# The activation buffers act_hi and act_lo moved up by 23872 bytes in each partition, the small buffers down by 32768

## What is computed

```
h = rmsnorm(x); x = x + nsa_pool_mixer(h, ...)      # q, k, v panels, three attention branches, pooling
x = x + swiglu(rmsnorm(x), w_gate, w_up, w_down)    # hidden width 2816
x = x + conformer_conv(rmsnorm(x), ...)             # 1024 -> 2048, depthwise conv of 31, layernorm, 1024 -> 1024
x = x + swiglu(rmsnorm(x), ...)
x = rmsnorm(x)                                      # end of the first block
u = _rmsnorm(h); proj = u @ w_in                    # q, k, v, g, and three conv inputs
h = h + concat([gla(...), conv(...)]) @ w_out
h = h + (silu(a) * b) @ w_down                      # a, b = _rmsnorm(h) @ w_gate_upffn
h = h + sigmoid(_rmsnorm(h) @ w_ple_gate) * (p @ w_ple_proj)
return _rmsnorm(h)
```

## Time and profile before

| | us |
|---|---|
| median of 3 runs | 1786.94 |
| lowest and highest | 1786.29 to 1790.84 |
| the profiled execution, its own time | 1790.93 |
| its span, first to last instruction | 1789.1 |
| PE busy | 1734.1 (97%) |
| DVE busy | 1251.9 (70%) |
| ACT busy | 867.4 (48%) |
| POOL busy | 516.9 (29%) |
| granted TensorE clock, mean | 0.979 |

### The profile page before, as it was taken

The page is one execution under the profiler, slowest core; times in us unless marked ns, Lnnn a source line. Parts: engine busy times, 40 slices in busy tenths (PEclk is TensorE's granted clock), DMA queues, the critical chain, the costliest instruction groups (busy, mean ns, idle before and its releaser), DMA issues.

```text
span 1789.1 us, 27531 instructions
## 1 busy us (share of the span) xinstructions
PE 1734.1 (97%) x10662; PEld 1498.1 (84%) x10662; DVE 1251.9 (70%) x1756; ACT 867.4 (48%) x1310; POOL 516.9 (29%) x356
## 2 busy tenths in 40 slices
PE   8999999999999999899999999999999999999997
PEld 6777788988998866689988998788788998899876
DVE  8667677754785798688744776678857875477575
ACT  5337556732773322456732763443335673277342
POOL 1342115502540246225502540012301550254000
PEclk9798999999999999899999999999999999999998
DMA  6210133333333465223333332422212333333332
GB/s 214 82 47 1 62 81 95 95 107 106 95 91 98 120 153 145 74 80 95 99 103 106 95 103 87 123 72 71 71 64 78 95 95 106 106 95 94 107 93 72
DMA packets 284699, 169.01 MB, mean 94 GB/s; under 512 B 8288, under 2 KB 278528, under 8 KB 284576
## 3 DMA queue, kind: packets, MB, share of 16 engines
q1 hardware_dynamic: 283664, 165.10, 32.7%
q0 software_dynamic: 624, 1.67, 0.3%
q10 hardware_dynamic: 288, 0.54, 0.1%
HBM read 156.59 MB, written 2.10 MB: 89 GB/s over the span
## 4 chain that ended last, share of the span: by engine, by line
PE 47%; DVE 6%; issue 1%; ACT 1%; POOL 0%; DVEq 0%; POOLq 0%; ACTq 0%
PE ps L1342 21%; PE ps L1027 8%; PE ps L1028 8%; PE ps L1029 8%; DVE wlo L1646 1%; DVE rstd L1688 1%; PE ps L1535 0%; ACT whi L602 0%; DVE act_lo L1678 0%; DVE act_lo L1676 0%; DVE wlo L1959 0%; DVE tt L1975 0%; DVE x L2439 0%; DVE bt_lo L1676 0%; DVE at L2305 0%
## 5 line engine op out<-in xcount | busy, mean ns | idle before, releaser
L1027 PE MATMUL ps<-act_hi,whi 128*128 128x512 f32 x796 | 320.0, 402 | 16.9 <-DVE act_lo L1678 8.8
L1028 PE MATMUL ps<-act_lo,whi 128*128 128x512 f32 x796 | 313.8, 394 | 0.0
L1029 PE MATMUL ps<-act_hi,wlo 128*128 128x512 f32 x796 | 313.0, 393 | 0.0
L602 ACT ACTIVATE whi<-raw 128x2048 fp32r<-128x2048 f32 (+3 forms) x104 | 167.0, 1606 | 233.7 <-PE ps L1029 219.4
L1646 DVE TENSOR_TENSOR wlo<-raw,whi 128x2048 fp32r<-128x2048 f32 (+3 forms) x96 | 191.3, 1993 | 42.7 <-ACT whi L602 42.5
L1342 PE MATMUL ps<-act_hi,whi 128*128 128x256 f32 x720 | 205.5, 285 | 11.2 <-ACT ps L773 6.9
L1027 PE MATMUL ps<-hid_hi,whi 128*128 128x512 f32 x528 | 209.8, 397 | 0.0
L1028 PE MATMUL ps<-hid_lo,whi 128*128 128x512 f32 x528 | 209.8, 397 | 0.0
L1029 PE MATMUL ps<-hid_hi,wlo 128*128 128x512 f32 x528 | 209.8, 397 | 0.0
L444 POOL TENSOR_TENSOR raw<-raw 128x512 f32<-128x512 f32 x60 | 82.3, 1372 | 437.5 <-DVE sqacc L1666 178.4
L1342 PE MATMUL ps<-act_hi,wlo 128*128 128x256 f32 x720 | 204.1, 283 | 0.0
(11 more groups left out here) (402 smaller groups left out, 3921.8 us busy)
## 6 DMA issues: line engine op xcount, KB each, us to landing
raw<-in_ffn_w_gate_dram SPq DMA_DIRECT2D x44, 512.0 KB, 3.9
raw<-in_ffn_w_up_dram SPq DMA_DIRECT2D x44, 512.0 KB, 5.1
raw<-in_w_gate_upffn_dram SPq DMA_DIRECT2D x44, 512.0 KB, 4.8
raw<-in_ffn_w_down_dram SPq DMA_DIRECT2D x32, 384.0 KB, 4.1
raw<-in_conv_w_pw_dram SPq DMA_DIRECT2D x24, 512.0 KB, 5.6
raw<-in_w_in_dram SPq DMA_DIRECT2D x24, 512.0 KB, 4.6
raw<-in_ffn_w_down_dram SPq DMA_DIRECT2D x32, 320.0 KB, 3.6
z<-z SPq DMA_DIRECT2D x28, 262.0 KB, 4.9
```

The lines of the kernel that those rows point to most:

```text
L602: act.activation(whi[:, n % 2, 0:cols], raw[:, n % 2, 0:cols], ACT.Copy).then_inc(hi_done, 1)
L1027: pe.matmul(out, lhs[0], rhs[0], start=start, stop=False)
L1028: pe.matmul(out, lhs[0], rhs[1], start=False, stop=False)
L1029: return pe.matmul(out, lhs[1], rhs[0], start=False, stop=stop)
```

## The change

act_hi and act_lo are named behind the small tiles, not ahead of them. No instruction is added, removed or moved: the instructions of every engine stand in the same order with the same operands, and only addresses differ.

```
         x = sb("x", [P, KD, S])
-        act_hi = sb("act_hi", [P, KD, S], F32R)
-        act_lo = sb("act_lo", [P, KD, S], F32R)
         rstd = sb("rstd", [P, S])
         sq = sb("sq", [P, 2, S])
         sqacc = sb("sqacc", [P, S])
...
         t2 = sb("t2", [P, 2, S])
         t3 = sb("t3", [P, 2, S])
         wtap = sb("wtap", [P, 2, CONV])
+        act_hi = sb("act_hi", [P, KD, S], F32R)
+        act_lo = sb("act_lo", [P, KD, S], F32R)
```

## The result

The changed kernel takes 1772.62 us (median of 5 runs, 1770.64 to 1772.95), the kernel before 1786.29 us in the same comparison. The ratio is 0.9928 with a 95% interval of 0.9917 to 0.9940: faster by 13.7 us, where 12.2 us slower was forecast.

A forecast was written before the change was run, and what follows sets the result against it. The prediction took TensorE, busy 1734.1 of 1789.1 us, to bound the kernel through its start-to-start matmul distances. 13.7 + 0 + 0 - 1.5 = +12.2 us on 1786.94 gave 1799.1 us, range 1785.5 to 1806.

The forecast's parts named there:

- start remainders: Start addresses of moving data and weights set a stream's pace; act, given hid's remainder 448, slows from 226.7 to 233.3 ns.
- height: Alternative cause: the border at byte 131072 counts; only act_lo from k = 4 crosses it, at most +2.6 us.
- takes hid's pace: 512-column matmuls on act (L1027 to L1029), given hid's remainder, go from a mean of 227.3 to 233.3 ns.
- to bt's value: 256-column products (L1342): act with whi goes from 119.2 to 118.3 ns, act with sw from 115.0 to 118.9.
- Part 1: 512-column matmuls on act (L1027 to L1029): 2289 of them lose 6.0 ns each, +13.7 us.
- Part 2: 256-column products (L1342): -1.9 us on whi and +2.8 us on sw, taken as 0, ends -2 to +3.
- Part 3: ScalarE and VectorE writes of act and the moved small buffers: no dearer, cost 0.
- Part 4: PE waits behind act streams (L1535, L1646, L1676): longer panels shorten them, -1.5 us, between 0 and -6.
- The one called faster: Unlike remainders are good: 2160 act products on whi gain 4.2 ns each, -9 us, giving 1777; chance 0.06.
- The rival that nothing happens: hid is slower for another reason than its remainder, so the kernel stays at 1787 to 1790; chance 0.22.
- the signs looked for: L1027 median 389 to 397 ns, 173 matmuls at 210 to 250 us, act with whi 283 to 280, hid stretches unmoved.

## Why the prediction was wrong

**The cause was right in part, its price and sign were not.** The forecast rested on start remainders as against height, and the runs confirm that: 64 bytes give all of the gain (1771.97) and moving to the top without them none (1784.43). The step that failed is the one from the rows to a price: that a placement has one pace, so that act, placed like hid, "takes hid's pace" and, with 256 columns, goes "to bt's value", while hid and bt keep theirs. One pair has two paces, and the runs showed act at the faster of the two and hid and bt going to it.

**Part 1** took 233.3 ns from hid and gave +13.7 us. It was 229.1 and +4.3 us. 233.3 is one of two patterns of that difference. Each of hid's six streams began behind act on whi with like starts, at 120, and stood in it; with no other engine at work the same pair stood at 233 and at 229, by what came before.

**Part 2** took 118.3 for act on whi from bt on whi, 12 matmuls between streams of another kind, and gave 0. It was 113.9 and -11.2 us, and with +3.3 for act on sw -7.9, the largest term of all. The two terms of act together are -3.6 us, so the sign of the sum was lost here. bt on whi was no measure of act on whi: its stretch came behind act on whi at 120 in every unit and stood in the pattern of 117.8. Why act on whi, behind bt on sw that also runs at 120, takes 113.3 is not shown.

**What was in no part.** The sum has terms for act alone. But hid (-7.0 us), bt on whi (-3.0) and bt on sw (+0.7) changed with nothing of theirs moved, -9.3 us in all, for which the sum had no term. I had read that distances drift for a few matmuls after a change of stream, and put it into a mean; that the pattern then taken can last for hundreds of matmuls did not occur to me. bt's 118.3 and act on sw's 115.0, both of unlike starts, were no sign of it: their differences are +64 and -64, two pairs and not one.

**Part 3** held: ScalarE's write of act_hi is 626 ns as before, VectorE's of act_lo has a median of 747 against 746 (L1678), and the small buffers' move gives nothing that a measurement could tell. **Part 4** was empty: the act streams ahead of the waits grew by 1.8 ns a matmul and not 6, 0.3 us over the 192 ahead of the qkd waits, and the waits stayed (3.0 against 3.2) or grew (5.0 against 4.2).

**The rivals.** The one called faster, with unlike starts as the good pairing, had the mechanism: products on whi gain more than the long streams lose. It gave 1777 and a chance of 0.06, against the measured 1772.6, and it had no term for hid either, so that it came so near is in part luck. What I held against it, bt on whi at 118.3 and hid as the slowest of all, was in both cases the other pattern of the same pair. The rival that nothing happens falls: 64 bytes in a start address are worth 13 us here. With it falls, for these streams, the distance that the Trainium skill states (page "TensorE: Matmul & The Clock Gate", section "Step-by-step: what each phase is for"), the column count, 213 ns: with no other engine at work streams of 512 columns take 226.7, 228.9 or 233.3. Whether the two read ports that the page names are what interferes, no run here shows. The rule of the Trainium skill that PE waits for nobody (page "SBUF — State Buffer", section "Who interferes with whom") is about other engines, and these runs don't speak against it: the excess is there without them. Of the signs looked for, "products of act with sw_hi go from 276 to 282" came out (283). The other numbers did not: 392 for 397, 175 for 173, 276 for 280, and the hid stretches did move.

## What to carry to other kernels

If TensorE is the bound, compare the distance from start to start of streams that differ only in the tiles they read; where it differs, put unused bytes ahead of one tile and time it, since neither the code nor the order has to change. Here weights and moving data that start 64 bytes apart suit streams of 256 columns (with the moving data 64 before the weights the fast pattern was met most often), and like starts, modulo 256, suit those of 512. Don't take the distance of one stretch as the price of a pair: a pair can have two. Expect streams whose tiles you didn't touch to change with their neighbours, and look at single stretches before you trust a mean: 116.6 was a mixture of 113.4 and 117.8.

## What was not expected of the hardware

- With rounded float32 operands and a new strip of weights for each matmul, a stream's distance depends on the difference of the start addresses of moving data and weights, with 256 alike to 0 and 32, 64, 96 and 128 not: 226.7, 228.9 or 233.3 ns with 512 columns, 113.3 to 120.0 with 256.
- Two patterns for one pair, 228.9 or 233.3 and 113.4 or 117.8. With 256 columns a pattern is kept from matmul to matmul, also across tiles with the same difference, until TensorE is held up (318.54 us in the changed kernel) or the difference changes. The stream before has a part in which one is taken; the rest of that rule is open.
- At a granted clock of 0.50 the distance was 427 ns for 512 columns, nothing above the column count.
- What the reads do to each other inside is open: no run shows it, only the sums.
